# Mixture-of-experts stage: two experts at a time on halves of TensorE's array, plain float32 on raw weights, 15 weight slots

## What is computed

```python
def hier_moe(h, w_rg, b_rg, w_re, b_re, w_eg, w_eu, w_ed):
    xt = h.reshape(n_tok, dm)
    lg = (xt @ w_rg + b_rg).astype(jnp.float32)
    grp = jnp.argmax(lg, axis=-1)                      # one of 4 groups
    ...
    top_p, top_i = lax.top_k(jax.nn.softmax(le, axis=-1), TOPK_IN_GROUP)   # 2 of its 8 experts
    gate = top_p / jnp.sum(top_p, axis=-1, keepdims=True) * p_grp
    expert = (grp[:, None] * EXPERTS_PER_GROUP + top_i).reshape(n_asg)
    ...
    def expert_block(args):
        xb, e = args
        return (jax.nn.silu(xb @ w_eg[e]) * (xb @ w_eu[e])) @ w_ed[e]
```

## Time and profile before

| | us |
|---|---|
| median of 3 runs (lowest, highest) | 2326.18 (2324.93, 2326.35) |
| profiled execution, span from first to last instruction | 2329.0 |
| stage "rt", from SP's first expert piece to the first expert product | 428.1 to 454.4 |
| stage "ex", to the last expert product | 454.4 to 999.3 |
| TensorE busy, share of the span | 2235.9, 96% |
| VectorE, ScalarE busy | 1801.5, 1161.0 |

### The profile page before, as it was taken

The page is one execution under the profiler, slowest core; times in us unless marked ns, Lnnn a source line. Parts: engine busy times, 40 slices in busy tenths (PEclk is TensorE's granted clock), DMA queues, the critical chain, the costliest instruction groups (busy, mean ns, idle before and its releaser), DMA issues. The chain is left out here.

```text
span 2329.0 us, 30346 instructions
## 1 busy us (share of the span) xinstructions
PE 2235.9 (96%) x11961; PEld 1898.9 (82%) x11961; DVE 1801.5 (77%) x2133; ACT 1161.0 (50%) x1215; POOL 138.8 (6%) x237
## 2 busy tenths in 40 slices
PE   7999989999999999999999999999998999999997
PEld 7888768788888888888788887888987888887886
DVE  6887687688989889866888777887796887776545
ACT  4443244577677776744444364333653333464332
POOL 2000100000000000000111001110001111000000
PEclk9999998999999999999999999999999999999999
DMA  8854553499999999954799536994633998445652
GB/s 300 272 138 148 177 172 100 154 375 375 368 372 375 363 376 363 364 165 154 228 373 350 165 114 210 375 349 169 208 127 112 333 357 289 141 129 166 196 181 72
DMA packets 346769, 567.83 MB, mean 244 GB/s; under 512 B 69248, under 2 KB 182400, under 8 KB 346624
## 3 DMA queue, kind: packets, MB, share of 16 engines
q1 hardware_dynamic: 325632, 490.31, 62.0%
q0 software_dynamic: 20992, 75.54, 8.7%
HBM read 564.71 MB, written 1.05 MB: 243 GB/s over the span
## 5 line engine op out<-in xcount | busy, mean ns | idle before, releaser
L321 PE MATMUL ps<-st_hi,sb_h_hi 128*128 128x512 f32 (+1 forms) x728 | 272.1, 374 | 11.7 <-DVE sb_h_lo L1187 4.6
L323 PE MATMUL ps<-st_hi,sb_h_lo 128*128 128x512 f32 (+1 forms) x728 | 265.0, 364 | 0.0
L322 PE MATMUL ps<-st_lo,sb_h_hi 128*128 128x512 f32 (+1 forms) x728 | 264.8, 364 | 0.0
L293 DVE TENSOR_TENSOR es_lo<-es_raw,es_hi 128x2048 fp32r<-128x2048 f32 x87 | 196.9, 2284 | 19.3 <-ACT es_hi L283 18.9
L321 PE MATMUL ps<-ring_hi,sb_h_hi 128*128 128x512 f32 (+1 forms) x504 | 191.2, 379 | 4.2 <-DVE sb_h_lo L832 2.1
L323 PE MATMUL ps<-ring_hi,sb_h_lo 128*128 128x512 f32 (+1 forms) x504 | 188.5, 374 | 0.0
L322 PE MATMUL ps<-ring_lo,sb_h_hi 128*128 128x512 f32 (+1 forms) x504 | 188.2, 373 | 0.0
L293 DVE TENSOR_TENSOR ring_lo<-ring_raw,ring_hi 128x2048 fp32r<-128x2048 f32 (+4 forms) x86 | 155.2, 1806 | 39.8 <-ACT ring_hi L283 39.7
L293 DVE TENSOR_TENSOR st_lo<-ring_raw,st_hi 128x2048 fp32r<-128x2048 f32 (+1 forms) x66 | 148.9, 2255 | 42.8 <-ACT st_hi L283 42.8
L283 ACT CAST es_hi<-es_raw 128x2048 fp32r<-128x2048 f32 x87 | 164.6, 1914 | 23.9 <-DMA es_raw<-in_w_expert_up_dram 17.9
L293 DVE TENSOR_TENSOR st_lo<-st_raw,st_hi 128x2048 fp32r<-128x2048 f32 x64 | 146.3, 2288 | 30.9 <-ACT st_hi L283 30.8
(11 more groups left out here) (798 smaller groups left out, 5383.6 us busy)
## 6 DMA issues: line engine op xcount, KB each, us to landing
t_aw<-in_ada_w_dram POOLq DMA_DIRECT2D x144, 512.0 KB, 6.6
st_raw<-in_ffn_w_in_dram SPq DMA_DIRECT2D x90, 512.0 KB, 5.8
ring_raw<-in_ffn_w_in_dram SPq DMA_DIRECT2D x86, 512.0 KB, 6.0
es_raw<-in_w_expert_gate_dram SPq DMA_DIRECT2D x40, 1024.0 KB, 8.2
es_raw<-in_w_expert_down_dram SPq DMA_DIRECT2D x39, 1024.0 KB, 7.4
es_raw<-in_w_expert_up_dram SPq DMA_DIRECT2D x37, 1024.0 KB, 7.4
ring_raw<-in_w_expert_up_dram SPq DMA_DIRECT2D x27, 1024.0 KB, 7.2
ring_raw<-in_w_expert_down_dram SPq DMA_DIRECT2D x25, 1024.0 KB, 7.2
```

Source lines behind the costliest of these rows:

```text
L293: dve.tensor_tensor(p.at(self.lo[m % self.held]), p.at(self.raw[n % self.slots]), p.at(self.hi[m % self.held]).bitcast(F32), ALU.subtract) ...
L321: pe.matmul(out, a_hi, b_hi, start=start, stop=False, skip_group_check=True)
L322: pe.matmul(out, a_hi, b_lo, start=False, stop=False, skip_group_check=True)
L323: return pe.matmul(out, a_lo, b_hi, start=False, stop=stop, skip_group_check=True)
```

## The change

1. **Pairs on halves.** Experts go two at a time, 16 pairs. Each has 64 slots: the tokens of expert 2p occupy columns 0 to 63 of the stationary operand, those of 2p+1 columns 64 to 127, and a product of one expert writes 64 partitions of PSUM (`ps[h * SL:(h + 1) * SL, ...]`). Products of the two experts alternate.
2. **Plain float32.** The product is one float32 matmul on the raw weights; nothing of the expert weights is split (`Piece(..., True)`), and there are no hi and lo buffers in this stream.
3. **Long runs.** Partition p holds rows 8p to 8p+7 of gate and up and 4p to 4p+3 of down, so each piece is one run of 8 KB a partition. The tokens' features, the router's weights and the hidden units are taken with strides of 8 and 4 to match.
4. **15 raw slots** in place of 5; a slot is free when its products are done. Three of them are opened, and sent, in stage "mx" behind that stage's own pieces; 12 more pieces follow in "rt".
5. **Routing by expert.** Ranks are counted for 32 experts at once. Units of four experts (two pairs) are placed, gathered, turned and given their gates one after the other: unit 0 in "rt", the seven others (`draw`) between the products of "ex".
6. **Each pair returns its own sum**: 16 scatters in place of 4.

The overflow pass (`late_programs`) is rewritten for experts with over 64 tokens and stands behind the same kind of test.

```diff
 def expert_plan(A):
-    deep = lambda w: w.rearrange("(k p) n -> p k n", p=P)
-            pieces += [Piece(deep(w[e, a * P:(a + 4) * P, :]), 4, BANK) for w in (wg, wu) for a in (0, 4)]
-            pieces += [Piece(deep(wd[e - 1, u * HB:(u + 1) * HB, :]), 2, 1024) for u in range(2)]
+    deep = lambda w: w.rearrange("(p k) n -> p k n", p=P)
+            pieces += [Piece(deep(w[e])[:, a:a + 4, :], 4, BANK, True)
+                       for w in (wg, wu) for a in (0, 4) for e in (2 * p, 2 * p + 1)]
+            pieces += [Piece(deep(wd[e])[:, f:f + 2, :], 2, 1024, True) for f in (0, 2) for e in (2 * p - 2, 2 * p - 1)]
+def gather(pe, M, out, perm, c):
+    for i in (2 * c, 2 * c + 1):
+        for w in range(2):
+            for t in range(2):
+                last = pe.matmul(out[:, i % 2 * 256:(i % 2 + 1) * 256], (M.h_hi, M.h_lo)[w][:, t, i:1024:8],
+                                 perm[:, t].rearrange("p x s -> p (x s)"), start=w == t == 0, stop=w == t == 1,
+                                 skip_group_check=True)
 def experts(k, A, M):
-            def half(e, bank, a):
-                w = S.take(pe)
+            def half(p, bank, a):
+                w = [S.take(pe), S.take(pe)]
                 for kt in range(a, a + 4):
-                    last = product(pe, ps[:, bank, :], M.hg_hi[:, e // NE, kt, :], M.hg_lo[:, e // NE, kt, :],
-                                   w[0][:, kt - a, :], w[1][:, kt - a, :], kt == 0, kt == 7)
+                    for h in range(2):
+                        at = (p % 2 * 2 + h) * SL
+                        last = pe.matmul(ps[h * SL:(h + 1) * SL, bank, :], M.hg[p // 2 % 2][:, kt, at:at + SL],
+                                         w[h][:, kt - a, :], start=kt == 0, stop=kt == 7, skip_group_check=True)
...
+            for p in range(NP):
+                v = unit_of(p)
+                if p:
+                    pe.wait_ge(silued, p)
+                half(p, 0, 0)
+                if p:
+                    turn(p - 1)
+                if v:
+                    draw(v, 3 * (p % 2))
+                half(p, 0, 4)
+                if p >= 2:
+                    scatter(p - 2, 0)
+                if p:
+                    pe.wait_ge(made, p)
+                half(p, 1, 0)
+                if v:
+                    draw(v, 3 * (p % 2) + 1)
+                if p >= 2:
+                    scatter(p - 2, 1)
+                half(p, 1, 4)
+                if p:
+                    down(p - 1, 0)
+                if v:
+                    draw(v, 3 * (p % 2) + 2)
+                if p:
+                    down(p - 1, 1)
...
+            scatter(NP - 2, 0)
+            down(NP - 1, 0)
+            scatter(NP - 2, 1)
+            down(NP - 1, 1)
 def moe_block(k, A, site):
-        k.stream = Stream(nc, "es", expert_plan(A), UNIT, k.shared, (None, None, 0, 1, None), (0, None, None, None)).place(own)
+        k.stream = k.experts.place(own)
...
         @block.sync
         def _(sp):
             S.send(sp, len(S.pieces))
+            k.experts.send(sp, 3)
...
+            k.experts = Stream(nc, "es", expert_plan(A), UNIT, k.shared, (None,) * 13 + (0, 1), ()).place(k.far, "right", 3)
```

More of the change, by code:

```diff
@@ L1420, in route @@
[L1420 to L1423, removed]
+        wr, br = k.wr, k.br
+        lt, rest, hit, one, two = (sb(n, [P, NT * R, NE]) for n in ("lt", "rest", "hit", "one", "two"))
+        asg, both = sb("asg", [P, NT, NG, NE]), sb("both", [P, NT, NG, NE])
+        m1, m2, b1 = (sb(n, [P, NT * R]) for n in ("m1", "m2", "b1"))
+        desc, ss, zg = sb("desc", [P, NE]), sb("ss", [P, NT]), sb("zg", [P, NT])
@@ L1612, in _ @@
[L1612 to L1622 removed]
+            after(dve.tensor_tensor(both[:], one_e, wide(w1[:]), ALU.mult))
@@ L1847, in program @@
-            copy(n * U + 1, 1)
-        guarded(act, found, program)
-    def vector_pass(dve, found):
-        def take(kind, b, u):
-            dve.wait_ge(high[kind], b + 1)
-            dve.tensor_tensor(lo[kind], raw[u][kind], hi[kind].bitcast(F32), ALU.subtract
-                              ).then_inc(split[kind], 1)
-        def expert(i, n, m, j, final=False):
-            for u in range(U):
-                b = n * U + u
-                more = not (final and u == 1)
-                if more:
-                    take(G, b + 1, 1 - u)
@@ L1904, in vector_pass, with program @@
+            dve.tensor_tensor(X[:, m, :], X[:, m, :], ps[:, 4:6, :].rearrange("p c n -> p (c n)"), ALU.add
+                              ).then_inc(kept, 1)
+        def program():
+            dve.memset(zero, 0.0).then_inc(cleared, 1)
+            for m in range(NT):
+                steps(dve, m, expert)
+            keep(NT - 1)
+            dve.wait_ge(kept, NT)
         guarded(dve, found, program)
@@ L1945, in _ @@
             for n in range(2):
-                sp.wait_ge(S.split, S.order[len(S.pieces) - 5 + n] + 1)
+                slot = S.slots - 2 + n
+                final = max(m for m in range(len(S.pieces)) if m % S.slots == slot)
+                sp.wait_ge(S.used, final + 1)
                 N2.send(sp, n + 1)
@@ L2015, in _ @@
+            turn(NP - 1)
+            for c in range(2):
+                last = pe.matmul(ps[:, c, :], k.ones[:], k.gates[:, 1, c * BANK:(c + 1) * BANK], start=True, stop=True)
+            last.then_inc(row_summed, 1)
+            found = first_of(pe)
+            scatter(NP - 2, 0)
+            down(NP - 1, 0)
+            scatter(NP - 2, 1)
+            down(NP - 1, 1)
             late_tensor(pe, found)
-            pe.wait_ge(added, 4 * (NG - 1))
+            pe.wait_ge(added, 4 * (NP - 1))
@@ new lines, in keep @@
+            def keep(p):
+                act.wait_ge(S.used, ends["down", p])
+                if p:
+                    act.wait_ge(spread, 4 * p)
+                act.copy(y_hi, ps[:, 4:6, :].rearrange("p c n -> p (c n)")).then_inc(raised, 1)
+            for p in range(NP):
+                v = unit_of(p)
+                if p:
+                    copy(p - 1)
+                if v:
+                    take(v, 3 * (p % 2))
+                act.wait_ge(S.used, ends["gate", p])
+                if p:
+                    act.wait_ge(made, p)
+                act.activation(silu[:], ps[:, 0, :], ACT.Silu).then_inc(silued, 1)
+                if v:
+                    take(v, 3 * (p % 2) + 1)
+                    take(v, 3 * (p % 2) + 2)
+                if p:
+                    keep(p - 1)
```

745 lines of the change are left out of this document (315 added, 430 removed).

## The result

The changed kernel takes 2239.68 us (median of 4 runs, 2234.7 to 2241.73) beside 2326.26 for the kernel before (4 runs, 2324.93 to 2328.67): a ratio of 0.9621, 95% interval 0.9608 to 0.9635, 86.6 us less. The forecast of 2267.5 had the direction and the bound right.

A forecast was written before the change was run, and what follows sets the result against it. TensorE and DMA both bound the kernel before, DMA alone afterwards. Last byte at 936.3 plus 3.4 and 0.9 gives 940.6 in place of 999.3, 58.7 us off the 2326.2 median: 2267.5 us, range 2240 to 2321.

The forecast's parts named there:

- The bound: Expert stage: DMA bounds afterwards, TensorE needing 26 us a pair and waiting in each for DMA's 32; chance 0.60.
- The rate: Expert stage's transfers: 198.2 MB at 390 GB/s take 508 us, last byte at 936; ends 353 and 399 GB/s.
- The opening claim: Expert stage before: TensorE (16.8 us an expert) and DMA (16.9) both limit, so easing either alone gains almost nothing.
- The two stretches by packet size: Trace of before: 2.0 KB packets ran at 393 GB/s, 3.6 KB at 333, so longer runs had no proven gain.
- long runs are faster: Rival on the expert stage's transfers: at 410 GB/s the last byte lands at 912, time 2243 us; chance 0.10.
- The sum by that figure, 2226: Whole kernel: at the skill's 425 GB/s the pieces take 466 us, giving 2226 us in place of 2267.5.
- Halves: Expert products on TensorE: full overlap by columns, a pair's 48 products taking 20.5 us in place of 41.
- The overlap of c = 1.59: Expert products: partial overlap as rival, TensorE staying the bound; at c = 1.6 stage ends at 960, 2287 us; chance 0.12.
- TensorE's pair: TensorE in the expert stage: 26 us a pair, 420 us in all, with gather products of 256 columns at 0.12 us.
- The tail: Stage's end after the last byte: four pairs of products, 3.4 us, and 0.9 for last scatter and landing.
- the 32 us of cover: Routing: twelve pieces filling the remaining slots keep DMA busy 32 us, to 460; first products start near 454.
- the drops priced at nothing: TensorE's clock in the expert stage: short pauses may drop it to 1.2 GHz; nothing within, at most 3 us at end.

The follow-up runs named there:

- the contiguous gathers: Changed kernel with features laid out tile by tile, so gathers load stationary operands without stride; 2239.93 us, ratio 0.9627.
- the early pieces: Changed kernel without the three pieces sent in the mixer's output, all 15 sent in routing; 2247.88 us, ratio 0.966.
- before with long runs: Kernel before with runs of 8 KB a partition and nothing else, features not reordered to match; 2326.5 us, ratio 0.9998.
- three pieces under way: Changed kernel with contiguous gathers, an expert piece issued only once the one three places ahead has landed; 2245.28 us, one run.
- the runs with idle splits: Changed kernel with contiguous gathers and 12 slots, plus copies and subtractions on an unused buffer, heavy and light; 2397.07 and 2317.68 us.

## Why the prediction was wrong, and where it was right

**The bound.** Right: with TensorE eased, DMA sets the end. Shown by the contiguous gathers (TensorE 7% lighter, no gain; then 29.9 us a pair, the pace of the transfers) and by the early pieces (DMA 7.5 us later, 8.2 us lost). That TensorE would wait in each pair did not come: it waited only from 835 on.

**The rate, the step that failed.** I took 390 GB/s between ends of 353 and 399; it is 421. 189 pieces then take 471 us in place of 508, 37 us, and this term took the time out of the range. The step failed in how it read "DMA's share is 1.02 at 371" as DMA's limit. It was TensorE's demand, as before with long runs shows; the lower end and the value were worked out from stretches that TensorE paced, and for the upper end, 399 from 40 to 60 us, no run shows what limited it. The opening claim, that an easier TensorE alone gains almost nothing in the stage, falls with it: with the runs of before and TensorE eased DMA does 394. (An expert's 6.29 MB at 371 GB/s are 17.0 us, not 16.9; nothing hangs on it.) The two stretches by packet size that I set against each other, 393 and 333, were four microseconds each of such a stream, and their order was the wrong way round: longer runs are faster, 394, 409, 421. The rival "long runs are faster" was thus the case, at 0.10 too little, and its 410 still too low. The reason I gave for 390 over 371, that the deep queue leaves no holes, is refuted: three pieces under way reach 419. The Trainium skill's figure, "HBM Reference", section Specifications (TRN2), about 425 GB/s for a core alone, agrees with the 421 of the trace. The sum by that figure, 2226, would have been 14 us too low.

**Halves.** Right, 20.9 us for a pair's products (six blocks of 3.49, as from 717.93 to 721.42) against 20.5 foretold. The overlap of c = 1.59 that was worked out from the Trainium skill, "TensorE: Matmul & The Clock Gate", Part 3 (2.38 times for three column tiles), is not what two tiles of 64 columns show here: 48 products at 0.86 are 41.3 us one after the other, and 41.3 / 20.9 is 1.97.

**TensorE's pair.** 28.4 us, not 26: a gather product of 256 columns costs 0.24 us (two records from 726.01 to 726.50), not the 0.12 of the earlier trace rows. That row has contiguous operands. It cost nothing only because DMA's 29.9 us stayed above; 5% more rate and TensorE would have been the bound.

**The tail.** Its size was right, its way in part luck. 4.3 us from the last byte to the end was foretold; the last landing is at 901.9 and the end at 907.4, 5.5 us on. But the working counted eight products right behind the last byte, and TensorE was not ready for them. The last landing that it waited for is the one before 892.12. From there on it works without a break for 15.3 us, through a down product, transposes, a row sum, a scatter, and the last pair's two down products with a scatter between; it comes to the last of them at 903.76, 1.8 us behind the landing.

**The ends of the transfer.** The forecast put nothing for them. From the first issue behind the border to the last landing, 425.01 to 901.9, the 189 pieces took 476.9 us, 6 more than at 421 GB/s throughout. Near the end the rate is down:

```profile
900.00:902.00 2.00, 2.00 (x12) 0.66 (x10) 0.00 (x0) 0.00 (x0) 0.00 (x0) 1.00 0.59 226
```

How much of the 6 us is due to the second block's two pieces (issued from 878.81), which share DMA with the last ones, and how much to starting and landing, was not measured.

**Routing, early pieces, what follows.** The early pieces went out at 398.45 into an idle stretch and were worth what was said. The first expert product came 23.5 us behind the first issue after the border (448.52), 26.3 before; the 32 us of cover held, as 428 to 454 at a share of 1.01 shows. The stages' gain was kept to the end: 88.8 us in the profile, 86.6 in the medians, and the second block's first product came 9.4 us behind the stages' end, 9.6 before. The granted clock stayed at 1.00 from 480 to 880, so the drops priced at nothing did not come here; in the runs with idle splits, where TensorE waited for other engines, the mean from 480 to 880 was 0.87 and 0.90.

**The sum in its own terms:** 512.5 us were foretold for the two stages (428.1 to 940.6), 508.2 for the pieces and 4.3 for the tail. Less 37.5 for the rate, 6.2 more for the ends of the transfer and 1.2 more for the tail gives the 482.4 of the profile.

## What to carry over

A DMA share near 1.00 does not say that DMA is at its limit while another engine paces it: take the rate from a stretch in which that engine demonstrably waits for landings, or keep the range open upwards. Lay weights out so that each partition reads one long run, since in this kernel that alone moved 394 to 421 GB/s; slots beyond a few serve to fill idle time ahead of a stage, not to raise the rate. Two products on different column halves cost the time of one if the list alternates them, and a stationary operand with a stride of eight loaded at a bit over half the speed.

## What was not expected of the hardware

- Rate by run length, one core, 1 MB pieces, queue full: 394 GB/s (2 and 4 KB), 409 (4 KB), 421 (8 KB), and no less with three pieces under way (419).
- The share of busy time is above 1 for short packets (1.04 at 394) and 1.01 at 421, and at a demand of 372 it still reads 0.97.
- A 128x128 weight load in fp32r with a stride of eight elements took 338 ns, a contiguous one 189, and the products behind it 0.24 us in place of 0.12.
- A product listed behind four others of the other half started ahead of one of them, beside the third; a full overlap needed the alternating list (28.4 us a pair against 35.6).
